# Feed-forward up phase as Strassen block products, with its rows through DRAM and the down phase in three chunks

## The reference

```
D_MODEL = 1024; SEQ = 1024; D_FF = 3 * D_MODEL; FFN_CONV = 3

h = rms_norm(x, g_ffn_pre[l])
up = h @ w_up[l]                                  # (1024, 1024) @ (1024, 6144)
gate_h = causal_dwconv(up[..., :D_FF], ffn_conv_w[l], ffn_conv_b[l])
hid = jax.nn.gelu(gate_h) * up[..., D_FF:]
x = x + rms_norm(hid @ w_down[l], g_ffn_post[l])  # (1024, 3072) @ (3072, 1024)
```

## Time and profile before

| | |
|---|---|
| median of 3 runs | 3303.26 us (3301.67 to 3303.79) |
| span of the profiled execution | 3301.3 us |
| PE busy | 3133.8 us (95%) |
| DVE busy | 2168.8 us (66%) |
| ACT busy | 1330.0 us (40%) |
| POOL busy | 998.0 us (30%) |

### The profile page before, as it was taken

How to read it: one execution, slowest core, us unless ns; L and a number is a source line. 1 busy time by engine, 2 the same in 40 slices (tenths; PEclk the granted TensorE clock), 3 DMA queues, 4 the chain that set the end, 5 groups by cost and what they waited for, 6 DMA issues and landing times.

```text
span 3301.3 us, 44691 instructions
## 1 busy us (share of the span) xinstructions
PE 3133.8 (95%) x15149; PEld 2503.4 (76%) x15149; DVE 2168.8 (66%) x2721; ACT 1330.0 (40%) x1772; POOL 998.0 (30%) x493
## 2 busy tenths in 40 slices
PE   6999998888997899999969999999999999999998
PEld 5668776565785788888858888888688888888877
DVE  7788977886545899999866775633654155144366
ACT  4345434667223788888740465101411010001142
POOL 2224332000342011111114433345144344344432
PEclk8999999999998899999989999999999999999999
DMA  7223221330343999999961222233211111111312
GB/s 261 71 64 90 64 70 45 116 116 26 98 146 115 384 382 378 380 385 380 336 234 51 76 77 77 78 111 113 81 45 46 50 49 46 51 45 51 108 39 70
DMA packets 351444, 446.17 MB, mean 135 GB/s; under 512 B 32942, under 2 KB 235612, under 8 KB 351332
## 3 DMA queue, kind: packets, MB, share of 16 engines
q1 hardware_dynamic: 336532, 410.05, 36.5%
q10 hardware_dynamic: 5440, 17.86, 1.7%
q0 software_dynamic: 9360, 16.80, 1.3%
HBM read 397.40 MB, written 58.75 MB: 138 GB/s over the span
## 4 chain that ended last, share of the span: by engine, by line
PE 57%; DVE 4%; SPq 3%; DMA 1%; issue 1%; ACT 1%; DVEq 0%; ACTq 0%; POOLq 0%
PE acc L430 14%; PE acc L432 14%; PE acc L431 14%; PE acc L2029 3%; PE acc L2031 3%; PE acc L2030 3%; PE acc L2050 1%; PE acc L2049 1%; PE acc L2048 1%; SPq L1932 1%; SPq L1933 1%; SPq L1936 1%; PE XX L2020 1%; DVE Al L709 0%; DMA mraw<-in_exp_w 0%
## 5 line engine op out<-in xcount | busy, mean ns | idle before, releaser
L430 PE MATMUL acc<-Ah,whi 128*128 128x512 f32 x2208 | 872.5, 395 | 7.6 <-DVE Al L718 3.2
L403 POOL TENSOR_TENSOR whi<-wraw,one 128x1024 fp32r<-128x1024 f32 (+1 forms) x199 | 377.4, 1897 | 1632.0 <-PE acc L432 1303.1
L432 PE MATMUL acc<-Ah,wlo 128*128 128x512 f32 x2208 | 860.9, 390 | 0.0
L431 PE MATMUL acc<-Al,whi 128*128 128x512 f32 x2208 | 860.9, 390 | 0.0
L405 POOL TENSOR_TENSOR wlo<-wraw,whi 128x1024 fp32r<-128x1024 f32 (+1 forms) x199 | 518.4, 2605 | 15.6
L430 PEld LDWEIGHTS acc<-Ah,whi 128*128 128x128 f32 x2208 | 414.6, 188 | 114.2 <-issue 16.4
L431 PEld LDWEIGHTS acc<-Al,whi 128*128 128x128 f32 x2208 | 414.9, 188 | 89.5 <-issue 4.1
L432 PEld LDWEIGHTS acc<-Ah,wlo 128*128 128x128 f32 x2208 | 414.7, 188 | 88.0
L2142 DVE TENSOR_TENSOR mlo<-mraw,mhi 128x1024 fp32r<-128x1024 f32 x256 | 306.9, 1222 | 37.3 <-ACT mhi L2086 24.6
L2086 ACT ACTIVATE mhi<-mraw 128x1024 fp32r<-128x1024 f32 x256 | 267.9, 1062 | 72.8 <-PE acc L2031 51.4
L430 PE MATMUL acc<-Bh,whi 128*128 128x512 f32 x640 | 249.9, 391 | 0.0
(11 more groups left out here) (598 smaller groups left out, 5008.4 us busy)
## 6 DMA issues: line engine op xcount, KB each, us to landing
mraw<-in_exp_w SPq DMA_DIRECT2D x512, 256.0 KB, 6.4
mraw<-in_exp_w SPq DMA_DIRECT2D x128, 512.0 KB, 11.6
wraw<-in_w_in SPq DMA_DIRECT2D x72, 512.0 KB, 3.8
wraw<-in_w_up SPq DMA_DIRECT2D x46, 512.0 KB, 3.8
TT<-in_ada_w SPq DMA_DIRECT2D x32, 512.0 KB, 3.9
TT<-gates SPq DMA_DIRECT2D x32, 512.0 KB, 4.4
wraw<-in_w_down SPq DMA_DIRECT2D x24, 512.0 KB, 3.9
adaraw<-in_ada_w SPq DMA_DIRECT2D x16, 512.0 KB, 10.2
```

The lines of the kernel that those rows point to most:

```text
L403: ch(pool.tensor_tensor(hi[:, r, 0:k, 0:m], wraw[:, r, 0:k, 0:m], one[:, 0:1].unsqueeze(2).broadcast_to([P, k, m]), ALU.mult))
L430: pe.matmul(o, hi[:, hr, j, 0:m], ih[:, k0 + j, cols], start=(j == 0), stop=False)
L431: pe.matmul(o, hi[:, hr, j, 0:m], il[:, k0 + j, cols], start=False, stop=False)
L432: last = pe.matmul(o, lo[:, hr, j, 0:m], ih[:, k0 + j, cols], start=False, stop=(j == k - 1))
```

## The change

The up phase is done pair by pair as one Strassen-Winograd product of 2 x 2 blocks. The block rows of a pair are the gate tile and the value tile, the inner dimension is cut into rows 0 to 3 and 4 to 7, and the tokens into halves. With weight blocks a11, a12 (gate), a21, a22 (value) and row blocks X11, X12, X21, X22 there are seven parts, each of 4 steps x 3 = 12 matmuls, so 84 where there were 96:

- Weights: part 0 a11, part 1 a21+a22-a11, part 2 a21+a22, part 3 a11-a21, part 4 a12, part 5 a12-(a21+a22-a11), part 6 a22. T1 to T4 are sums of row blocks, made once. Parts 4, 5 and 6 add into the banks of parts 0, 2 and 3 after DVE has read these.
- POOL sums the weights (`early_sums`, `late_sums`, into US) and makes one low part (`last_low`); ACT makes all seven high parts (`weight_high`), DVE six low parts (`weight_low`). This is done for pair n + 1 while pair n runs: there is one buffer for the seven, and each is overwritten once its part has been used.
- DVE folds the parts (ue, uf, ug, uu) and does the convolution and the products as before. `u_used` counts PE's parts, `u_mid` DVE's folds, `up_done` finished pairs; the accumulators are two sets of four banks.
- The hidden rows, high and low, are stored to DRAM (`hid_store`) and loaded again in three chunks of 8 (`hid_load`) into Ah/Al and Bh/Bl in turn for the down products, which come after the whole up phase. X3, PR, PL, BG and the rows of the last norm change places in memory.
- Pair 0 takes the parts in the order 0, 4, 2, 5, 3, 1, 6 as rows come; POOL makes its weights between the splits for w_o. After the rows of the second half DVE also makes T1 to T4 and their low parts (16 and 16 instructions), ACT their high parts.

```diff
+    UWH = alloc("UWH", [P, 7, 4, P], F32R, offset=o_bl)
+    UWL = alloc("UWL", [P, 7, 4, P], F32R, offset=o_bl + 14336)
+    US = alloc("US", [P, 2, 4, P], F32, offset=o_bl + 28672)
+    uraw = [alloc("uraw0", [P, 2, KD, P], F32, offset=o_c), wraw]
...
+    T2h = alloc("T2h", [P, 4, HALF], F32R, offset=o_bh)
...
+    hidTh = dram("hidTh", [D_FF, T])
+    hidTl = dram("hidTl", [D_FF, T])
...
+    def quarters(raw):
+        return raw[:, 0, 0:4, :], raw[:, 0, 4:8, :], raw[:, 1, 0:4, :], raw[:, 1, 4:8, :]
+    def early_sums(pool, m, odd):
+        a11, a12, a21, a22 = quarters(uraw[odd])
+        pool.wait_ge(S("u_lo"), 6 * m)
+        pool.tensor_tensor(US1, a21, a22, ALU.add).then_inc(S("u_sums"), 1)
+        pool.wait_ge(S("u_sums"), 4 * m + 1)
+        pool.tensor_tensor(US2, US1, a11, ALU.subtract).then_inc(S("u_sums"), 1)
+    def late_sums(pool, m, odd):
+        a11, a12, a21, a22 = quarters(uraw[odd])
+        pool.wait_ge(S("u_lo"), 6 * m + 3)
+        pool.tensor_tensor(US1, a11, a21, ALU.subtract).then_inc(S("u_sums"), 1)
+        pool.wait_ge(S("u_lo"), 6 * m + 4)
+        pool.wait_ge(S("u_sums"), 4 * m + 2)
+        pool.tensor_tensor(US1, a12, US2, ALU.subtract).then_inc(S("u_sums"), 1)
+    def last_low(pool, m, odd):
+        pool.wait_ge(S("u_hi"), 7 * m + 7)
+        pool.tensor_tensor(UWL[:, 6, :, :], quarters(uraw[odd])[3], UWH[:, 6, :, :].bitcast(F32), ALU.subtract)\
+            .then_inc(S("u_last_lo"), 1)
...
+        with pool.Fori(0, 11) as i:
+            for r in range(2):
+                m = 2 * i + 1 + r
+                late_sums(pool, m, 1 - r)
+                pool.wait_ge(S(f"uraw{r}"), 32 * i + 32 + 32 * r)
+                early_sums(pool, m + 1, r)
+                last_low(pool, m, 1 - r)
+        late_sums(pool, UP_PAIRS - 1, 1)
+        last_low(pool, UP_PAIRS - 1, 1)
...
+    XT1, XT3, XT2, XT4 = (tuple(f) for f in zip(T_hi, T_lo))
+    UBANKS = [[acc[0][:, lo_tok], acc[0][:, hi_tok], acc[1][:, lo_tok], acc[1][:, hi_tok]],
+              [X[0], X[1], Y[:, lo_tok], Y[:, hi_tok]]]
...
+    def weight_source(i, raw):
+        a11, a12, a21, a22 = quarters(raw)
+        return (a11, US2, US1, US1, a12, US1, a22)[i]
+    def weight_high(act, m, i, odd, used):
+        act.wait_ge(S("u_used"), used)
+        if i in (1, 2, 3, 5):
+            act.wait_ge(S("u_sums"), 4 * m + {2: 1, 1: 2, 3: 3, 5: 4}[i])
+        act.activation(UWH[:, i, :, :], weight_source(i, uraw[odd]), ACT.Copy).then_inc(S("u_hi"), 1)
+    def weight_low(dve, m, i, odd):
+        dve.wait_ge(S("u_hi"), 7 * m + i + 1)
+        dve.tensor_tensor(UWL[:, i, :, :], weight_source(i, uraw[odd]), UWH[:, i, :, :].bitcast(F32), ALU.subtract)\
+           .then_inc(S("u_lo"), 1)
...
+        def pair(n, p, land=None):
+            act.wait_ge(S("u_used"), 7 * n + 1)
+            act.activation(up1[p][:], UBANKS[p][0], ACT.Copy).then_inc(S("u_p1"), 1)
+            if land is not None:
+                act.wait_ge(S(f"uraw{1 - p}"), land)
+                weight_high(act, n + 1, 0, 1 - p, 7 * n + 1)
+            gelu(act, n - 1, 1 - p)
+            if land is not None:
+                weight_high(act, n + 1, 1, 1 - p, 7 * n + 2)
+            hidden_high(act, n - 1, 1 - p)
+            if land is not None:
+                for i in range(2, 7):
+                    weight_high(act, n + 1, i, 1 - p, 7 * n + i + 1)
...
+        def t1(k):
+            dve.wait_ge(S("n5_scaled"), KD + k + 1)
+            dve.tensor_tensor(C[:, k, lo_tok], C[:, k, hi_tok], C[:, k, lo_tok], ALU.subtract).then_inc(S("t_sum"), 1)
...
+        def sum_low(q, k):
+            dve.wait_ge(S("t_hi"), 4 * q + k + 1)
+            dve.tensor_tensor(T_lo[q](k), T_sum[q](k), T_hi[q](k).bitcast(F32), ALU.subtract).then_inc(S("t_lo"), 1)
...
+        def conv(n, p, stored):
+            g = hidden(p)
+            dve.wait_ge(S(f"hid_st{p}"), stored)
+            ch(dve.tensor_scalar(g, ug[:], vecd("ffn_conv_w_2", n + 48), vecd("ffn_conv_b_2", n), ALU.mult, ALU.add))
+            for back in range(1, 3):
+                ch(dve.scalar_tensor_tensor(g[:, back:], ug[:, 0:T - back], vecd("ffn_conv_w_2", n + 24 * (2 - back)),
+                                            g[:, back:], ALU.mult, ALU.add))
+            dve.sem_inc(S("conv"), 1)
+        def second_half(n, p, step):
+            if step == 0:
+                ch(dve.tensor_tensor(uu[:], uu[:], R5, ALU.mult))
+            if step == 1:
+                dve.wait_ge(S("gelu"), n + 1)
+                ch(dve.tensor_tensor(hidden(p), hidden(p), uu[:], ALU.mult))
+                dve.sem_inc(S("hid"), 1)
+            if step == 2:
+                dve.wait_ge(S("hid_hi"), n + 1)
+                dve.tensor_tensor(hidden(p), hidden(p), hidh[p][:].bitcast(F32), ALU.subtract).then_inc(S("hid_lo"), 1)
...
+        def pair(n, p, stored, weights=True):
+            a, b, c, d = UBANKS[p]
+            if weights:
+                weight_low(dve, n + 1, 0, 1 - p)
+            second_half(n - 1, 1 - p, 0)
+            dve.wait_ge(S("u_used"), 7 * n + 2)
+            dve.wait_ge(S("u_p1"), n + 1)
+            dve.tensor_tensor(ue[:], up1[p][:], b, ALU.add).then_inc(S("u_mid"), 1)
+            if weights:
+                weight_low(dve, n + 1, 1, 1 - p)
+            second_half(n - 1, 1 - p, 1)
+            dve.wait_ge(S("u_mid"), 3 * n + 1)
+            dve.wait_ge(S("u_used"), 7 * n + 3)
+            dve.tensor_tensor(uf[:], c, ue[:], ALU.add).then_inc(S("u_mid"), 1)
+            if weights:
+                weight_low(dve, n + 1, 2, 1 - p)
+            second_half(n - 1, 1 - p, 2)
+            dve.wait_ge(S("u_mid"), 3 * n + 2)
+            dve.wait_ge(S("u_used"), 7 * n + 4)
+            dve.tensor_tensor(uu[:, hi_tok], d, uf[:], ALU.add).then_inc(S("u_mid"), 1)
+            if weights:
+                weight_low(dve, n + 1, 3, 1 - p)
+            dve.wait_ge(S("u_used"), 7 * n + 5)
+            ch(dve.tensor_tensor(ug[:, lo_tok], a, R5h[0], ALU.mult))
+            if weights:
+                weight_low(dve, n + 1, 4, 1 - p)
+            dve.wait_ge(S("u_used"), 7 * n + 6)
+            ch(dve.tensor_tensor(ug[:, hi_tok], c, ue[:], ALU.add))
+            if weights:
+                weight_low(dve, n + 1, 5, 1 - p)
+            ch(dve.tensor_tensor(ug[:, hi_tok], ug[:, hi_tok], R5h[1], ALU.mult))
+            conv(n, p, stored)
+            dve.wait_ge(S("u_used"), 7 * n + 7)
+            ch(dve.tensor_tensor(uu[:, lo_tok], d, ue[:], ALU.add))
+            dve.sem_inc(S("up_done"), 1)
+        with dve.Fori(0, 11) as i:
+            for r in range(2):
+                pair(2 * i + 1 + r, 1 - r, 32 * i + 32 + 32 * r)
...
+    def hid_store(sp, n, p):
+        sp.wait_ge(S("hid_lo"), n + 1)
+        sp.dma_start(hidTh[ds(n * P, P), :], hidh[p][:].bitcast(F32)).then_inc(S(f"hid_st{p}"), 16)
+        sp.dma_start(hidTl[ds(n * P, P), :], hidden(p)).then_inc(S(f"hid_st{p}"), 16)
+    def hid_load(sp, c, k):
+        dst = ((Ah, Al), (Bh, Bl))[c % 2]
+        for t, src in zip(dst, (hidTh, hidTl)):
+            sp.dma_start(t[:, k, :].bitcast(F32), src[(c * KD + k) * P:(c * KD + k + 1) * P, :]).then_inc(S(f"hid_in{c % 2}_{k}"), 16)
...
+        sp.wait_ge(S("u_lo"), 6 * UP_PAIRS)
+        sp.wait_ge(S("u_last_lo"), UP_PAIRS)
+        for m in range(2):
+            load(sp, N0["down0"] + m, m, WDN[:, 0:KD, m * P:(m + 1) * P])
+        hid_stored(sp, 0)
+        sp.wait_ge(S("u_used"), LAST + 3)
+        for k in range(4):
+            hid_load(sp, 0, k)
+        hid_store(sp, UP_PAIRS - 2, 0)
+        sp.wait_ge(S("u_used"), LAST + 6)
+        for k in range(4, KD):
+            hid_load(sp, 0, k)
...
+        def part(i, bank, x, start, ready=None, after=None):
+            for k in range(4):
+                if ready is not None:
+                    pe.wait_ge(S(ready[0]), ready[1] + k + 1)
+                pe.matmul(bank, UWH[:, i, k, :], x[0](k), start=(start and k == 0), stop=False, skip_group_check=not start)
+                pe.matmul(bank, UWH[:, i, k, :], x[1](k), start=False, stop=False, skip_group_check=not start)
+                last = pe.matmul(bank, UWL[:, i, k, :], x[0](k), start=False, stop=(k == 3), skip_group_check=not start)
+                if k == 3:
+                    last.then_inc(S("u_used"), 1)
+                if after is not None:
+                    after(k)
...
+        first = [(0, a, X11, ("n5_lo", 0), square(0, 0)), (4, X[0], X21, ("n5_lo", 4), square(0, 4)),
+                 (2, c, XT1, ("t_lo", 0), square(1, 0)), (5, X[1], X22, ("n5_lo", 8), square(1, 4)),
+                 (3, d, XT3, ("t_lo", 4), None), (1, b, XT2, ("t_lo", 8), None), (6, Y[:, lo_tok], XT4, ("t_lo", 12), None)]
...
+        def pair(n, p, second=False):
+            a, b, c, d = UBANKS[p]
+            if second:
+                pe.wait_ge(S("x_read"), 1)
+            else:
+                pe.wait_ge(S("up_done"), n - 1)
+            pe.wait_ge(S("u_lo"), 6 * n + 1)
+            part(0, a, X11, True)
```

(34 more changed lines are left out.)

390 lines of the change are left out of this document (260 added, 130 removed).

## The result

The changed kernel takes **3337.55 us** as the median of four runs (3332.86 to 3339.43), against 3303.18 for the kernel before: a ratio of 1.0103 (1.0090 to 1.0117). Predicted were 3344 us, in a range of 3305 to 3366, and slower. The profiled execution took 3332.86 us, the lowest of the four, with a span of 3331.1.

A forecast was written before the change was run, and what follows sets the result against it. DVE's queue, with port waits against POOL and waits for ACT, was taken to bound the up phase at 22.5 us a pair. Stages from 2403 to 3192.8 gave +40.5 on 3301.3, 3341.8; plus 2.0, 3344 us, range 3305 to 3366.

The forecast's parts named there:

- DVE's own 17.3 us: Up phase, each pair: DVE's 19 instructions, hand-offs and loop turn take 17.3 us, under PE's 19.04.
- Port waits, 3.0 us: Up phase, each pair: DVE waits for POOL's port use, in the convolution and 0.5 at half 4, together 3.0 us.
- Waits for ACT, 0.9 and 1.3: Up phase, each pair: DVE waits 0.9 us before weight half 2 and 1.3 us before half 3.
- 22.5 us a pair: Up phase: DVE's time per pair, which PE waits for; 22.5 instead of 21.76 us, 21 times, +15.5 us.
- The first pair: Start of up: 64 DVE instructions of 0.76 us, 48.6 us, so pair 1 starts at 2403, +16 us.
- ACT: hidden: First pair: ACT's three operations per row take 2.1 us against DVE's 2.3, so they cost nothing.
- Pair 1: Second pair: part 4 comes 20 us after 2403, then three parts of 8.2 us; 28.5 instead of 21.76, +6.7.
- The entry to down: Between up and down: loads of hidden rows delay the first down product, +5 us, between 0 and 10.
- The low clock in the pairs costs nothing: Rival, up phase: low clock after waits adds 1.7 us to PE's 19.0, under DVE's 22.5; chance within a shared 0.08.
- What would show it: Changed profile: DVE and PE some 85% busy, multiply-adds 2.1 us, PE waiting some 2.5 us before every part 4.
- the first one: Rival, up phase: PE stays the bound at 19.04 us a pair, total 3268 us; chance 0.13.
- half of the port waits: Rival, up phase: POOL meets PSUM readers instead; 20.5 to 21.4 us a pair, 3296 to 3319 us; chance 0.11.

The follow-up runs named there:

- e1: Changed kernel with POOL's five instructions per pair on one column instead of 512 from pair 1 on, results wrong: 3272.25 us, ratio 0.9900.
- e6: Changed kernel plus third buffer for weight sums, convolution's first tap on ACT, R5 applied once behind down, and later hidden-row store: 3275.08 us, ratio 0.9919.
- e9: e6 plus ACT making the high part of a T1 row before squaring the next row, second half of tokens: 3268.90 us, ratio 0.9894.
- e11: Changed kernel with only POOL's two early sums and last low part on one column from pair 1 on, results wrong: 3286.25 us, ratio 0.9948.
- e2: Changed kernel with a third buffer for POOL's weight sums, so late sums may start one DVE step earlier: 3307.10 us, ratio 1.0008.
- e8: Changed kernel with ACT making the high part of a T1 row before squaring the next row, second half of tokens: 3331.23 us, ratio 1.0084.
- e5: Changed kernel with the store of pair 22's hidden rows issued behind the first chunk's loads of rows 4 to 7: 3335.67 us, ratio 1.0100.
- e10: Changed kernel with the two late sums and last low part made by DVE instead of POOL from pair 2 on: 3326.67 us, ratio 1.0069.
- e12: Changed kernel without loading low parts of hidden rows 4 to 7 of the first chunk, old ones used: 3335.14 us, ratio 1.0100.

## Why the prediction was right, point by point

- *PE's 19.04 us a pair*: right. It is seen where PE is the bound, 18.97 to 19.00 in e1, e6 and e9.
- *DVE's own 17.3 us*: right. 21.93 less 2.8 of port waits and less 1.9 for ACT (40.0 us in 21 pairs) leaves 17.2. Inside it the tensor_scalar was too short: e1 shows 0.81 us for it alone, not 0.68.
- *Port waits, 3.0 us*: 2.8 in the groups of e1 and after; 2.2 of them, those of the convolution, confirmed alone by e11 (predicted from the same rows: 2.5). The one at half 4 was put at 0.5 and is 0.59.
- *Waits for ACT, 0.9 and 1.3*: 0.70 and 1.24. The first was over-sized; e2 shows that the second is the late sum's.
- *22.5 us a pair*: 21.93 on DVE, 21.81 on PE. The over-sized waits make up most of the difference, which is 14.4 us over the 21 pairs. The last pair was put at 21.0 and took 19.6. Against that the first pair and the entry were put too low, by 8.1 us with pair 1, so that half of the 15.8 us too much was paid back by what was too little. The rest, with a first pair that began 2.8 us earlier than before's, makes the predicted span of 3341.8 10.7 us more than the profiled one; 3344 was 6.5 over the median. That the errors paid each other back is luck.
- *The first pair*: second pair predicted at 2403, seen at 2405.18, but in an execution whose first pair began 2.8 us earlier than before's. The stage is 20.9 us longer, not 16. The step that failed is "ACT: hidden". Its busy time is indeed below DVE's; its queue order made DVE wait 6.0 us in a ring, which a sum of busy times can't show, and e8 gave 5.2 back: its first pair is 15.7 us longer than before's, close to the 16 worked out without the ring.
- *Pair 1*: 28.5 predicted, 29.1 measured, but by two misses that cancel. Its part 4 came after 18.3 us (2423.47) instead of 20, and the three parts from there took 10.8 instead of 8.2, since most matmuls of part 4, behind a wait of 6.21 us, ran 0.43 us apart.
- *The entry to down*: +5 predicted on 261.2 + 1.6, and 270.4 − 262.8 = 7.6 measured; the first down product takes 18.4 us (to 2930.30) and not 16. The waits, 4.07 us, were sized about rightly; what was left out is the low clock behind the long one, 12 x (0.43 − 0.23) = 2.4 us. The row cited for the transfers gives only their sum, 13.7 us; the 2.76 us a MB agree with the 378 to 385 GB/s of the fullest slices on the page of the kernel before, and with e5's rows.
- *The low clock in the pairs costs nothing*: right for the time. From 2600 to 2605 us, behind a wait of 2.42 us, the clock is 0.71. On the mean PE needs 20.1 us for its 84 matmuls (21.81 less 1.68 of waiting) instead of 19.04, but DVE never waits for it. In e2, with no wait over 1.0 us, the clock is 1.00 in the whole stretch.
- *What would show it*: the long multiply-adds, the waits released by DVE and the spread first pair were there. PE's wait is not one of 2.5 us before every part 4, but 1.7 on the mean: a pair leaves PE 2.77 us and not 3.5, and slower matmuls, which the profile shows as busy, take 1.1 of them. So PE shows 92% busy, not 85.
- *Rivals*: e1 is the first one made true, and gives 3272 where 3268 was worked out. The 20.5 us of "half of the port waits" came with e2's buffer, not by itself. The break-even of 20.8 us a pair was put too high: e2 has 20.50 and is still not faster than the kernel before, since the first pair and the entry cost more than was allowed for.

Put together: on the 23 pairs behind the first, 12 matmuls less are worth 23 x 2.72 = 62.6 us. DVE's queue took 21 x 2.77 = 58.2 of it back, pair 1 10.1 and the last pair 0.5, which leaves +6.2 us. The first pair adds 20.9, the entry to down 7.6, and the low clock of 1.7 us behind before's wait is gone: +33.0. The profiled execution began this part 2.8 us earlier, so +30.2 at the end of down; the two timelines show 3182.32 against 3152.3, +30.0. The medians lie 34.4 us apart. The gain was real and went into DVE's queue; with the edits of e9 it comes out, and the kernel is 1.1% faster than the one before.

## What to carry to other kernels

When work moves off the bounding engine, lay out the queue of the engine that receives it in program order, with the port rule and every copy it waits for. Here that layout was right within 3% and a sum of busy times would have said "hidden". If such an engine misses its target by a little, look first for a buffer that lets a helper run one step earlier, for factors that can be applied once at the end, and for helper work that costs its owner no more than the waits it causes. For a stage with several engines also follow each queue for rings: the operation that waits longest may stand in front of one that nobody needed to delay.

## What the runs showed of the hardware

- VectorE's multiply-add of 1023 columns with both inputs in SBUF: 1283 ns with GpSimd's instructions on one column (e1), 2083 with a GpSimd instruction of 128x512 issued just before. Four of GpSimd's five instructions per pair cost VectorE 0.6 to 0.8 us each in this way; in e10 VectorE makes such a sum itself in 0.62 (L3092 starts at 2604.53, the next instruction at 2605.15). So here a GpSimd sum that meets such an instruction is no cheaper for VectorE than one of its own.
- TensorE's clock: one wait of 3.57 us was followed by 12 matmuls at 0.43 us each, the 1.2 GHz level, and in e12 one of 2.17 us by 6; four waits of 0.69 to 1.43 us in e5, 2.5 to 3.1 us apart and 3.84 us together, were followed by none. Two windows of the changed kernel, with the granted clock as the third number from the end; the first follows a wait of 2.42 us:

```profile
2600.00:2605.00 5.00, 5.00 (x17) 3.96 (x17) 3.63 (x5) 1.58 (x2) 2.02 (x1) 0.71 0.03 11
2620.00:2625.00 5.00, 4.48 (x19) 3.64 (x20) 3.99 (x6) 1.58 (x2) 0.32 (x1) 1.00 0.10 25
```

The second lies around a wait of 0.75 us that ends at 2620.52, and keeps the full clock, 2.4 GHz.
